# Loading the expert weights with each partition's rows 128 apart instead of adjacent, and transposing contiguous columns instead of strided ones

## The chip, the core and the metric

One Trainium2 chip, one core. The metric is the device time in microseconds of one execution of the whole program, median of the runs given.

## The reference, cut to what matters

The program computes two transformer-like blocks on 256 tokens of width 1024, all in float32. Only the last part of the second block is touched: a mixture of experts with 32 experts, of which each token uses 4.

```
def moe(h, router_w, router_b, w_up, b_up, w_down, b_down):
    logits = (xt @ router_w + router_b)
    top_vals, top_idx = lax.top_k(logits, TOP_K)          # 4 of 32
    gates = jax.nn.softmax(top_vals, axis=-1)
    ...
    def expert_block(args):                               # for each expert e and its tokens
        hcat = xblk @ w_up[e] + b_up[e]                   # [1024] -> [2048]
        x_glu = jnp.minimum(hcat[:, 0::2], SWIGLU_LIMIT)
        x_lin = jnp.clip(hcat[:, 1::2], -SWIGLU_LIMIT, SWIGLU_LIMIT)
        act = x_glu * jax.nn.sigmoid(SWIGLU_ALPHA * x_glu) * (x_lin + 1.0)
        return act @ w_down[e] + b_down[e]                # [1024] -> [1024]
```

Each expert has 8 MB of w_up and 4 MB of w_down, 402.7 MB over the 32 experts (192 panels of 2,097,152 bytes), and each byte is read once.

## The kernel before

Engines run side by side and meet at semaphores. All large weights pass through one ring in SBUF of six slots, each a "panel" of 2 MB (128 partitions of 16 KB). In the first 61 panels (the dense layers, four slots of the ring) a weight matrix is read as 512 columns, so that a partition's 16 KB come in eight pieces of 2 KB, or as 512 rows, in four pieces of 4 KB; both use the pattern `(k p) n -> p k n`, where the rows that one partition holds are 128 apart.

The expert stage (`moe_pe`, `moe_act`, `moe_dve`, `moe_sp`) is a hardware loop over e = 0 to 31 on each engine. An expert has six panels, j = 0 to 3 for w_up (256 rows of 2048 each) and j = 4, 5 for w_down (512 rows of 1024 each). SyncE issues them in that order at line 1923; before each it waits (line 1921) until TensorE has counted up `consumed` for the panel that held the slot. Here the rearrangement is `(p k) n`: partition p holds rows that are adjacent in the matrix, two of 8 KB or four of 4 KB, so 16 KB in one piece.

TensorE does for expert e, in this order (`dense`): the bias of the up product; the four up panels, 64 slots of tokens at a time, the two halves of the output on two halves of the array side by side (`halves`, lines 1535 and 1536); the gather of expert e+1's token rows; the first half of the scatter of expert e-1's result; four transposes of the activation `glu` (line 1522), whose first one also frees a slot; four transposes of the gathered rows of expert e+1 (line 1516); the first down panel; the second half of the scatter; the second down panel; two transposes of the weighted one-hot matrix (line 1529). ScalarE copies the transposed activation out of PSUM (line 1737) before the down product may start, and the transposed rows (line 1740) before the next expert's up product. A weight matrix laid out as `(p k)` needs inputs in the same order. So the transposes take every fourth column of `glu` and every second column of the rows: the columns that belong to panel row r. In a transpose the data is the weight load (PEld in the profile) and the identity matrix is the moving operand.

An expert that more than 64 tokens chose gets an extra pass over its panels (`one_pass`), during which no slot is freed until the pass is through with it. With these inputs that happens once, for expert 21.

The views and rows of the ring are made by these lines:

```
self.order = [4, 5] + [(PANELS + r) % RING for r in range(RING)]
self.panel = [k.ring[:, slot, :].rearrange("p (k n) -> p k n", k=2 if j < 4 else 4)
              for j, slot in enumerate(self.order)]
```

Of the kernel before, what the change touches and what calls it, by code (L numbers as in the profile page):

```python
# [21 lines left out]
P = 128  # L22
# [1479 lines left out]
def moe_pe(k, m):  # L1502
    nc, M, s = k.nc, k.nc.tensor, k.s

    def gather():

        for tt in range(TT):
            last = halves(m.XR, m.one_hot[:, tt, :], [k.x[:, tt, c:c + 512] for c in (0, 512)],
                          start=(tt == 0), stop=(tt == TT - 1))
        return last  # L1510

    def transpose_rows():

        for n in range(4):
            at = 256 * (n // 2) + n % 2
            last = M.transpose(m.XT[:, n * P:(n + 1) * P], m.xrows[:, at:at + 255:2], k.ident[:])
        return last

    def transpose_activated(frees):

        for n in range(4):
            last = M.transpose(m.AT[:, n * P:(n + 1) * P], m.glu[:, n::4], k.ident[:])  # L1522
            if n == 0 and frees:
                last.then_inc(s.consumed, 1)
        return last

    def transpose_weighted(frees):
        for tt in range(TT):
            last = M.transpose(m.AT[:, tt * P:(tt + 1) * P], m.weighted[:, tt, :], k.ident[:])
            if tt == 0 and frees:  # L1530
                last.then_inc(s.consumed, 1)
        return last
# [5 lines left out]
    def up_bias():  # L1538
        for q in range(2):
            halves(m.U[:, q, :], m.brow_of[:], [m.brow[:, c:c + 512] for c in (512 * q, D + 512 * q)],  # L1540
                   start=True, stop=False)

    def up_panel(inp, j):
        for r in range(2):
            for q in range(2):
                last = halves(m.U[:, q, :], inp[:, (2 * j + r) % 4, (2 * j + r) // 4, :],
                              [m.panel[j][:, r, c:c + 512] for c in (512 * q, D + 512 * q)],
                              start=False, stop=(j == 3 and r == 1))
        return last

    def down_panel(j):
        for r in range(4):
            c = 4 * j + r
            last = halves(m.DN, m.actT[:, r, j * SLOTS:(j + 1) * SLOTS],
                          [m.panel[4 + j][:, r, c0:c0 + 512] for c0 in (0, 512)], start=(c == 0), stop=(c == KD - 1))
        return last

    def scatter_tile(tt, matrix, rows):
        for half in range(2):
            r = slice(half * SLOTS, (half + 1) * SLOTS)  # L1560
            last = M.matmul(m.S[:, half, :], matrix[r, tt * P:(tt + 1) * P], rows[r, :], start=True, stop=True)  # L1561
        return last
# [8 lines left out]
    for tt in range(TT):  # L1571
        for c in range(KD):
            last = M.matmul(W[:, tt, 0:NE], k.hT[:, c, tt * P:(tt + 1) * P], m.rw[:, c, :], start=(c == 0), stop=(c == KD - 1))
# [10 lines left out]
    M.wait_ge(s.built, 2)  # L1584
    gather().then_inc(s.gathered, 1)
    M.wait_ge(s.rows_copied, 1)
    transpose_rows().then_inc(s.rows_T, 1)

    M.wait_ge(s.gate_ready, 1)
    for tt in range(TT):  # L1590
        last = M.transpose(m.S[0:NE, 0, tt * P:(tt + 1) * P], m.gate[:, tt, 0:NE], k.ident[:])
# [3 lines left out]
    for tt, ps in enumerate((m.S, k.psA[:, 2:4, :])):  # L1595
        for half in range(2):
            last = M.matmul(ps[:, half, :], m.gT[:, tt * P:(tt + 1) * P], m.bdown[:, half * 512:(half + 1) * 512],
                            start=True, stop=True)
# [5 lines left out]
    with M.Fori(0, NE) as e:  # L1604

        def panel_in(j):
            slot = m.order[j]
            before = 0 if slot >= RING else (PANELS - 1 - slot) // RING + 1
            M.wait_ge(s.panel_in[slot], 16 * (before + 1) + e * 16)

        def dense(free):
            M.wait_ge(s.gather_copied, 1 + e)
            M.wait_ge(s.u_taken, 1 + e)
            M.wait_ge(s.selected, 1 + e)
            up_bias()
            for j in range(3):
                panel_in(j)
                last = up_panel(m.xg, j)
                if free:
                    last.then_inc(s.consumed, 1)  # L1620
            panel_in(3)
            up_panel(m.xg, 3).then_inc(s.up_done, 1)
            M.wait_ge(s.built, 4 + e * 2)
            M.wait_ge(s.rows_copied, 1 + e)
            gather().then_inc(s.gathered, 1)
            M.wait_ge(s.y_copied, 1 + e)
            M.wait_ge(s.scatter_copied, 1 + e)
            M.wait_ge(s.summed, 1 + e * 2)
            scatter_tile(0, m.scatter, m.y).then_inc(s.scattered, 1)
            M.wait_ge(s.activated, 2 + e)  # L1630
            transpose_activated(free).then_inc(s.act_T, 1)
            M.wait_ge(s.rows_copied, 2 + e)
            transpose_rows().then_inc(s.rows_T, 1)
            M.wait_ge(s.act_copied, 2 + e)
            panel_in(4)
            last = down_panel(0)
            if free:
                last.then_inc(s.consumed, 1)
            M.wait_ge(s.summed, 2 + e * 2)
            scatter_tile(1, m.scatter, m.y).then_inc(s.scattered, 1)  # L1640
            panel_in(5)
            down_panel(1).then_inc(s.down_done, 1)
            M.wait_ge(s.gated, 3 + e * 2)
            transpose_weighted(free).then_inc(s.gated_T, 1)

        tokens = nc.values_load(m.cnt[0:1, bass.ds(e, 1)], min_val=0, max_val=T, engines=[M.engine])
        with M.If(tokens < SLOTS + 1):
            dense(True)
        with M.Else():
            dense(False)  # L1650

        def one_pass(i):
            dve_step = lambda n: extra_step(s, "dve", e, i, n)
            act_step = lambda n: extra_step(s, "act", e, i, n)

            def free_two(step):

                M.wait_ge(*extra_step(s, "pe", e, i, step))
                M.sem_inc(s.settled, 1)
                with M.If(tokens < 2 * SLOTS + 1):  # L1660
                    M.sem_inc(s.consumed, 2)

            M.wait_ge(*dve_step(2))
            gather().then_inc(s.extra_pe, 1)
            M.wait_ge(*act_step(1))
            transpose_rows().then_inc(s.extra_pe, 1)
            M.wait_ge(*dve_step(3))
            M.wait_ge(*act_step(2))
            up_bias()
            up_panel(m.xg_x, 0)  # L1670
            up_panel(m.xg_x, 1).then_inc(s.extra_pe, 1)
            free_two(3)
            up_panel(m.xg_x, 2)
            up_panel(m.xg_x, 3).then_inc(s.extra_pe, 1)
            free_two(4)
            M.wait_ge(*dve_step(7))
            transpose_activated(False).then_inc(s.extra_pe, 1)
            M.wait_ge(*act_step(4))
            down_panel(0)
            down_panel(1).then_inc(s.extra_pe, 1)  # L1680
            free_two(6)
            M.wait_ge(*dve_step(10))
            M.wait_ge(*act_step(5))
            transpose_weighted(False).then_inc(s.extra_pe, 1)
            M.wait_ge(*act_step(6))
            scatter_tile(0, m.scatter_x, m.y_x).then_inc(s.extra_pe, 1)
            M.wait_ge(*dve_step(11))
            scatter_tile(1, m.scatter_x, m.y_x).then_inc(s.extra_pe, 1)

        extra_passes(M, s, e, tokens, "pe", one_pass)  # L1690
        with M.If(tokens > 2 * SLOTS):
            M.sem_inc(s.consumed, 6)
# [218 lines left out]
def moe_sp(k, m):  # L1911
    S, s = k.nc.sync, k.s
    w_up, w_down = k.a["expert_w_up_2"][0], k.a["expert_w_down_2"][0]
    S.wait_ge(s.late, LATE_MOE)
    with S.Fori(0, NE) as e:
        for j, slot in enumerate(m.order):
            if j < 4:
                source = w_up[bass.ds(e, 1), j * 256:(j + 1) * 256, :]
            else:
                source = w_down[bass.ds(e, 1), (j - 4) * 512:(j - 3) * 512, :]  # L1920
            S.wait_ge(s.consumed, PANELS - 5 + j + e * 6)
            S.sem_inc(s.settled, 1)
            S.dma_start(m.panel[j], source.rearrange("o (p k) n -> p (o k) n", p=P)).then_inc(s.panel_in[slot], 16)
    for tt in range(TT):
        S.wait_ge(s.ln_done, 2 + tt + 1)
        S.dma_start(k.out[0, tt * P:(tt + 1) * P, :], m.acc[:, tt, :]).then_inc(s.stored, 16)
    S.wait_ge(s.stored, 16 * TT)


def build(nc, ctx, arrays, out):  # L1930
# [49 lines left out]
    moe_pool(k, m)  # L1980
    moe_act(k, m)
    moe_pe(k, m)
    moe_dve(k, m)
    moe_sp(k, m)


# [26 lines left out]
```

## Time and profile before

| what | value |
|---|---|
| median of 3 runs | 1999.52 us (1998.67 to 2000.78) |
| the profiled execution | 1998.67 us, of which 1997.4 us from the first to the last instruction (the span) |
| TensorE busy | 1861.5 us, 93% of the span |
| VectorE, ScalarE busy | 615.5 us, 463.9 us |
| mean granted TensorE clock | 0.967 of full speed |
| moved by DMA | 536.95 MB, mean 269 GB/s over the span |
| expert stage | from about 966 us to the end |

The busy time of an engine is an average over stages with different limits. A timeline gives for each merged row its start, its length, engine, line, operation, operands and count, and in brackets the idle time before it with what ended it. A window gives the busy time of each engine in a stretch with the count of its instructions, then the granted clock (1.00 is full speed), the mean busy share of the 16 DMA engines (it can read a little over 1) and the rate.

### The profile page before, as it was taken

What the parts mean: (1) busy time and instruction counts of PE and PEld (TensorE: products, weight loads), DVE (VectorE), ACT (ScalarE), POOL (GpSimd) and SP (SyncE); (2) the same over time, 40 slices, a digit from 0 to 9 for tenths busy, and PEclk for the clock granted to TensorE, in tenths of its full rate; (3) what the DMA queues carried; (4) which work ended last, traced back from release to release, by engine and by line L of the source; (5) the groups of instructions that cost most, each with busy time, mean ns of one, the idle gap of its engine ahead of it and who ended that gap; (6) DMA issues with size and microseconds to landing.
All of it is one profiled execution on the core that took longest, in us unless ns stands there. A gap on an engine that the chain in (4) does not pass through costs nothing.

```text
span 1997.4 us, 22265 instructions
## 1 busy us (share of the span) xinstructions
PE 1861.5 (93%) x8651; PEld 1002.2 (50%) x8652; DVE 615.5 (31%) x790; ACT 463.9 (23%) x556; POOL 53.8 (3%) x63
## 2 busy tenths in 40 slices
PE   7989998987999999998579999999999997999996
PEld 6769994474799877554323333333333332333332
DVE  4444442242544403551312212221222121222223
ACT  1435440131444313230101111111111110111111
POOL 0000001000000110220000000000000000000000
PEclk9989998999999999998689999999999998999998
DMA  7334543412354533230769999999999976999994
GB/s 259 142 138 170 207 171 99 155 43 81 130 197 183 174 126 119 92 127 0 305 270 429 429 428 429 428 429 429 428 429 429 428 311 252 395 429 429 428 429 180
DMA packets 84809, 536.95 MB, mean 269 GB/s; under 512 B 8688, under 2 KB 8792, under 8 KB 60152
## 3 DMA queue, kind: packets, MB, share of 16 engines
q1 hardware_dynamic: 79088, 531.64, 65.7%
q10 hardware_dynamic: 5672, 4.59, 0.9%
q8 instruction: 38, 0.62, 0.1%
q14 instruction: 11, 0.09, 0.0%
HBM read 535.17 MB, written 1.05 MB: 268 GB/s over the span
## 4 chain that ended last, share of the span: by engine, by line
PE 82%; DVE 8%; DMA 5%; ACT 2%; issue 2%; ACTq 0%; POOL 0%; PEldq 0%; DVEq 0%; SPq 0%; POOLq 0%
PE psA L1535 34%; PE psB L669 9%; PE psA L680 9%; PE psB L340 6%; PE psA L353 6%; PE psB L331 6%; DMA panel_ring<-in_expert_w_up 4%; PE psA L1065 2%; PE psB L1561 2%; PE psA L1522 1%; DVE linear L1866 1%; DVE glu L1869 1%; DVE glu L1863 1%; DVE linear L1864 1%; ACT activated_T L1737 1%
## 5 line engine op out<-in xcount | busy, mean ns | idle before, releaser
L1535 PE MATMUL psA<-panel_ring,gathered_T 128*64 128x512 f32 x1024 | 446.1, 593 | 2.4 <-DMA panel_ring<-in_expert_w_up 2.4
L1536 PE MATMUL psA<-panel_ring,gathered_T 128*64 128x512 f32 x1024 | 446.1, 593 | 0.0
L1535 PEld LDWEIGHTS psA<-panel_ring,gathered_T 128*64 128x64 f32 x1024 | 140.2, 137 | 296.8 <-issue 288.9
L1535 PE MATMUL psA<-panel_ring,activated_T 128*64 128x512 f32 x528 | 242.8, 603 | 7.3 <-ACT activated_T L1737 6.6
L1536 PE MATMUL psA<-panel_ring,activated_T 128*64 128x512 f32 x528 | 242.8, 603 | 0.0
L566 DVE TENSOR_TENSOR w_low<-panel_ring,w_high 128x2048 fp32r<-128x2048 f32 x64 | 146.5, 2292 | 171.8 <-ACT w_high L612 171.8
L1863 DVE TENSOR_SCALAR glu<-psA 128x512 f32<-128x512 f32 x32 | 22.1, 692 | 492.5 <-PE psA L1536 492.5
L612 ACT ACTIVATE w_high<-panel_ring 128x2048 fp32r<-128x2048 f32 x64 | 122.5, 1917 | 178.9 <-PE psB L669 104.9
L669 PE MATMUL psB<-hT_high,w_high 128*128 128x256 f32 x512 | 145.0, 283 | 2.0 <-DVE w_low L566 2.0
L669 PE MATMUL psB<-hT_low,w_high 128*128 128x256 f32 x512 | 144.9, 283 | 0.0
L669 PE MATMUL psB<-hT_high,w_low 128*128 128x256 f32 x512 | 144.9, 283 | 0.0
L1535 PEld LDWEIGHTS psA<-panel_ring,activated_T 128*64 128x64 f32 x528 | 67.5, 138 | 153.5 <-issue 139.7
L1536 PEld LDWEIGHTS psA<-panel_ring,gathered_T 128*64 128x64 f32 x1024 | 140.2, 137 | 0.0
L1819 DVE TENSOR_TENSOR moe_sum<-moe_sum,psB 128x1024 f32<-128x1024 f32 x68 | 82.8, 1218 | 168.7 <-PE psB L1561 168.7
L1732 ACT ACTIVATE swish_gate<-glu 128x512 f32<-128x512 f32 x32 | 20.1, 629 | 470.0 <-DVE glu L1863 470.0
L340 PE MATMUL psB<-panel_ring,hT 128*128 128x512 f32 x288 | 126.8, 601 | 1.3 <-DVE hT L304 1.3
L331 PE MATMUL psB<-hT,panel_ring 128*128 128x256 f32 x512 | 111.7, 379 | 2.7 <-DVE hT L1224 1.4
L331 PEld LDWEIGHTS psB<-hT,panel_ring 128*128 128x128 f32 x512 | 97.0, 190 | 16.5 <-DVE hT L1224 1.8
L669 PEld LDWEIGHTS psB<-hT_high,w_high 128*128 128x128 f32 x512 | 98.3, 192 | 3.8 <-issue 3.6
L680 PE MATMUL psA<-w_high,aT_high 128*128 128x512 f32 x256 | 99.7, 389 | 0.0
L680 PE MATMUL psA<-w_low,aT_high 128*128 128x512 f32 x256 | 99.7, 389 | 0.0
L680 PE MATMUL psA<-w_high,aT_low 128*128 128x512 f32 x256 | 99.6, 389 | 0.0
(392 smaller groups left out, 2375.9 us busy)
## 6 DMA issues: line engine op xcount, KB each, us to landing
panel_ring<-in_expert_w_up SPq DMA_DIRECT2D x128, 2048.0 KB, 14.8
panel_ring<-in_expert_w_down SPq DMA_DIRECT2D x64, 2048.0 KB, 15.0
panel_ring<-in_mlp_w SPq DMA_DIRECT2D x32, 2048.0 KB, 8.1
panel_ring<-in_w_in SPq DMA_DIRECT2D x11, 2048.0 KB, 7.9
panel_ring<-in_fox_w_in SPq DMA_DIRECT2D x6, 2048.0 KB, 7.8
panel_ring<-in_lru_w_in SPq DMA_DIRECT2D x4, 2048.0 KB, 16.8
panel_ring<-in_lru_w_out SPq DMA_DIRECT2D x2, 2048.0 KB, 7.8
panel_ring<-in_fox_w_out SPq DMA_DIRECT2D x2, 2048.0 KB, 8.6
```

What stands on the lines that cost most here:

```text
L331: last = M.matmul(out[:, m, :], w[:, c, m * P:(m + 1) * P], k.hT[:, c, :], start=(c == 0), stop=(c == KD - 1))
L340: last = M.matmul(ps[:, tt, :], k.hT[:, c, tt * P:(tt + 1) * P], w[:, c, :], start=(c == 0), stop=(c == KD - 1))
L353: mm = M.matmul(k.psA[:, 2 * tt + half, :], aT[:, c, tt * P:(tt + 1) * P], w[:, c, half * 512:(half + 1) * 512], start=first and c == 0, s ...
L566: rest = V.tensor_tensor(to(t.w[i % 2][1][:]), view, to(t.w[i % 2][0][:]).bitcast(F32), ALU.subtract)
L612: A.activation(to, view, ACT.Copy).then_inc(s.w_high, 1)
L669: last = M.matmul(out[:, 2 * (i % 2) + m, :], w[p][:, c, m * P:(m + 1) * P], h[q][:, c, :], start=(c == 0 and p == q), stop=(c == KD - 1 a ...
L680: last = M.matmul(k.psA[:, 2 * tt + half, :], at[p][:, 2 * (i % 2) + c, tt * P:(tt + 1) * P], w[q][:, c, half * 512:(half + 1) * 512], sta ...
L1065: last = M.matmul(ps[:, tt, :], k.hT[:, c, tt * P:(tt + 1) * P], wj[:, c, :], start=(c == 0), stop=(c == KD - 1))
L1535: M.matmul(ps[0:SLOTS], lhsT, rhs[0], **flags)
L1536: return M.matmul(ps[SLOTS:P], lhsT, rhs[1], **flags)
L1819: return V.tensor_tensor(m.acc[:, tt, :], m.acc[:, tt, :], flat(m.S[:]), ALU.add)
L1863: V.tensor_scalar(m.glu[:], even, SWIGLU_LIMIT, None, ALU.min).then_inc(s.glu_made, 1)
```

## The change

The expert panels are read with `(k p) n` instead of `(p k) n`: partition p now holds rows p and p+128 of the 256 rows of a w_up panel, and rows p, p+128, p+256, p+384 of the 512 rows of a w_down panel. The slot, the panel's size, the number of loads and their order stay as they were. The inputs of the products are put in the matching order by transposing contiguous blocks of 128 columns of the rows and of `glu`. The numbers of transposes, weight loads and matmuls, their shapes, and all waits stay as they were; two helper functions become one.

```
-    def transpose_rows():
-        for n in range(4):
-            at = 256 * (n // 2) + n % 2
-            last = M.transpose(m.XT[:, n * P:(n + 1) * P], m.xrows[:, at:at + 255:2], k.ident[:])
-        return last
-
-    def transpose_activated(frees):
-        for n in range(4):
-            last = M.transpose(m.AT[:, n * P:(n + 1) * P], m.glu[:, n::4], k.ident[:])
-            if n == 0 and frees:
-                last.then_inc(s.consumed, 1)
-        return last
+    def transposed(ps, src):
+        for n in range(4):
+            last = M.transpose(ps[:, n * P:(n + 1) * P], src[:, n * P:(n + 1) * P], k.ident[:])
+        return last
...
-            transpose_activated(free).then_inc(s.act_T, 1)
+            for n in range(4):
+                last = M.transpose(m.AT[:, n * P:(n + 1) * P], m.glu[:, n * P:(n + 1) * P], k.ident[:])
+                if free and n == 0:
+                    last.then_inc(s.consumed, 1)
+            last.then_inc(s.act_T, 1)
             M.wait_ge(s.rows_copied, 2 + e)
-            transpose_rows().then_inc(s.rows_T, 1)
+            transposed(m.XT, m.xrows).then_inc(s.rows_T, 1)
...
-            S.dma_start(m.panel[j], source.rearrange("o (p k) n -> p (o k) n", p=P)).then_inc(s.panel_in[slot], 16)
+            S.dma_start(m.panel[j], source.rearrange("o (k p) n -> p (o k) n", p=P)).then_inc(s.panel_in[slot], 16)
```

The calls ahead of the loop and in the extra pass are changed in the same way.

## Rows read from the trace of the kernel before

**Rows 1.** Page: PE busy time, and GB/s moved in 40 slices.
```profile
PE 1861.5 (93%) x8651; PEld 1002.2 (50%) x8652; DVE 615.5 (31%) x790; ACT 463.9 (23%) x556; POOL 53.8 (3%) x63
...
GB/s 259 142 138 170 207 171 99 155 43 81 130 197 183 174 126 119 92 127 0 305 270 429 429 428 429 428 429 429 428 429 429 428 311 252 395 429 429 428 429 180
```

**Rows 2.** Windows, one expert each: busy by engine, clock, DMA share, GB/s.
```profile
1301.90:1330.40 28.50, 28.22 (x132) 9.61 (x130) 6.21 (x11) 4.46 (x7) 0.00 (x0) 1.00 1.01 429
1559.80:1589.10 29.30, 28.43 (x132) 9.49 (x130) 6.20 (x11) 4.46 (x7) 0.00 (x0) 1.00 1.01 428
```

**Rows 3.** Timeline of the SyncE queue: start us, length, loads issued (merged).
```profile
1044.96 13.85 SPq L1923 DMA_DIRECT2D panel_ring<-in_expert_w_up  x4
...
1073.51 13.85 SPq L1923 DMA_DIRECT2D panel_ring<-in_expert_w_up  x4
...
1501.71 13.99 SPq L1923 DMA_DIRECT2D panel_ring<-in_expert_w_up  x4
...
1559.75 14.67 SPq L1923 DMA_DIRECT2D panel_ring<-in_expert_w_up  x4
...
1589.12 14.67 SPq L1923 DMA_DIRECT2D panel_ring<-in_expert_w_up  x4
...
1699.54 13.85 SPq L1923 DMA_DIRECT2D panel_ring<-in_expert_w_up  x4
```

**Rows 4.** Ring tile, the one issue at 1044.96: us from issue to landing.
```profile
DMA to landing us min/median/max: 7.5/7.5/7.5
```

**Rows 5.** Ring tile, the one issue near 1603.8: us from issue to landing.
```profile
DMA to landing us min/median/max: 22.2/22.2/22.2
```

**Rows 6.** Timeline of TensorE: the last matmul that a load released.
```profile
1625.70 0.64 PE L1535 MATMUL psA<-panel_ring,gathered_T 128*64 128x512 f32 x1 [0.60 <-DMA panel_ring<-in_expert_w_up]
```

**Rows 7.** Page: DMA packets by size.
```profile
DMA packets 84809, 536.95 MB, mean 269 GB/s; under 512 B 8688, under 2 KB 8792, under 8 KB 60152
```

**Rows 8.** Windows amid loading: four with 4 KB packets, two 2 KB, one 16 KB.
```profile
833.60:837.20 3.60, 3.60 (x10) 1.69 (x9) 3.40 (x2) 0.16 (x1) 3.36 (x1) 1.00 1.02 419
850.90:854.40 3.50, 3.50 (x10) 1.59 (x9) 3.30 (x2) 0.17 (x1) 3.25 (x1) 1.00 1.02 421
868.30:871.80 3.50, 3.50 (x10) 1.59 (x9) 3.39 (x2) 0.08 (x1) 3.35 (x1) 1.00 1.01 413
481.80:485.80 4.00, 4.00 (x11) 1.74 (x10) 0.00 (x0) 0.00 (x0) 0.00 (x0) 1.00 1.01 403
714.50:718.80 4.30, 4.30 (x22) 3.78 (x21) 0.00 (x0) 0.00 (x0) 0.00 (x0) 1.00 1.01 388
268.00:272.20 4.20, 4.20 (x38) 4.20 (x37) 2.29 (x1) 0.36 (x2) 0.00 (x0) 1.00 0.97 371
966.90:996.40 29.50, 18.96 (x75) 14.50 (x76) 11.78 (x34) 2.71 (x7) 0.00 (x0) 0.56 1.01 428
```

**Rows 9.** Groups of weight loads of transposes, expert stage: mean ns last before the bar.
```profile
L1516 PEld LDWEIGHTS psB<-ident,gathered_rows 128*128 128x128 f32 x132 | 18.8, 209 | 2.4 <-ACT gathered_rows L1750 2.4
L1522 PEld LDWEIGHTS psA<-ident,glu 128*128 128x128 f32 x132 | 18.6, 210 | 32.5 <-DVE glu L1869 28.6 <-DVE glu L1890 3.9
...
L1529 PEld LDWEIGHTS psA<-ident,gated_one_hot 128*128 128x128 f32 x66 | 6.6, 141 | 28.0 <-issue 26.0 <-ACT extra_out L1758 2.0
```

**Rows 10.** Timeline of one expert: transposes, copy, first down matmul.
```profile
1314.77 0.56 PEld L1522 LDWEIGHTS psA<-ident,glu 128*128 128x128 f32 x4 [0.90 <-DVE glu L1869]
...
1315.36 0.64 PE L1516 MATMUL psB<-ident,gathered_rows 128*128 128x128 f32 x4
...
1315.56 0.60 ACT L1737 ACTIVATE activated_T<-psA 128x512 f32<-128x512 f32 x1 [1.27 <-PE psA L1522]
...
1316.21 0.64 PE L1535 MATMUL psA<-panel_ring,activated_T 128*64 128x512 f32 x1 [0.21 <-ACT activated_T L1737]
```

**Rows 11.** Matmuls of two lines, 1300 to 1500: duration ns min/median/max.
```profile
L1522 PE MATMUL psA<-ident,glu x28: 283/285/386, 1314.8 to 1486.5; 128*128 128x128 f32 x28
...
L1529 PE MATMUL psA<-ident,gated_one_hot x14: 272/300/329, 1324.4 to 1495.9; 128*128 128x128 f32 x14
```

More of the change, by code:

```diff
@@ L1630, in dense @@
             M.wait_ge(s.activated, 2 + e)
-            transpose_activated(free).then_inc(s.act_T, 1)
+            for n in range(4):
[3 more added lines that the diff above has]
+            last.then_inc(s.act_T, 1)
             M.wait_ge(s.rows_copied, 2 + e)
-            transpose_rows().then_inc(s.rows_T, 1)
+            transposed(m.XT, m.xrows).then_inc(s.rows_T, 1)
             M.wait_ge(s.act_copied, 2 + e)
@@ L1665, in one_pass @@
             M.wait_ge(*act_step(1))
-            transpose_rows().then_inc(s.extra_pe, 1)
+            transposed(m.XT, m.xrows).then_inc(s.extra_pe, 1)
             M.wait_ge(*dve_step(3))
@@ L1676, in one_pass @@
             M.wait_ge(*dve_step(7))
-            transpose_activated(False).then_inc(s.extra_pe, 1)
+            transposed(m.AT, m.glu).then_inc(s.extra_pe, 1)
             M.wait_ge(*act_step(4))
```

## The prediction

> **What bounds the kernel now.** I read the page first. TensorE is busy 93% of the span, and over the expert stage the DMA rate stands flat at 428 to 429 GB/s [rows 1]. Two engines near their limit at once, so the busy shares cannot say which one sets the time. The windows of single experts can: an early one takes 28.50 us with TensorE busy for 28.22, a late one 29.30 us with TensorE busy for 28.43, and the DMA share is 1.01 in both [rows 2].
>
> The queue's timeline gives the exact periods. From the issue for expert 2 (1044.96) to that for expert 18 (1501.71) 16 periods pass, 28.547 us each. From 1559.75 to 1589.12 it is 29.37 us [rows 3]. A load of six panels is 12.583 MB; at 428.6 GB/s that is 29.36 us, 4.893 us a panel. So the DMA engines need 0.81 us more per expert than TensorE does, and the ring hides it at first. The landing times show how: with an idle queue a panel lands after 7.5 us [rows 4], late in the stage only after 22.2 us [rows 5]. Each expert adds 0.81 us of backlog until the six slots can hide no more. That cover is 16 x 0.81 plus about 0.7 in the 17th period: 13.7 us. From about expert 19 on TensorE waits for w_up panels; the last such wait ends at 1625.70 [rows 6].
>
> A check of this reading: the panel waited for there is up panel 3 of expert 21, the 118th from 1044.96 (19 experts of six and four more). 7.5 less one panel's 4.9 leaves 2.6 us of start; 1044.96 + 2.6 + 118 x 4.893 = 1624.9, and 1625.7 was seen. So up to there (segment A) the time is set by DMA alone, however fast TensorE is. Then expert 21's extra pass stops the loads, the queue runs empty, and expert 23's start at 1699.54 [rows 3] with full cover again. In segment B, the last 8.7 experts of loads, the backlog grows to 8.7 x 0.81 = 7.1 us, under 13.7. There TensorE sets the time.
>
> **Part 1, the loads: pieces of 8 and 4 KB in place of 16 KB.** The page counts 84809 packets, 60152 of them under 8 KB [rows 7]. The other 24657 are, within 81, the 192 x 128 = 24576 partitions of expert panels: one packet each. Afterwards a w_up panel has 256 packets and a w_down panel 512, that is 8 and 24 more for each of the 16 DMA engines. The order in HBM changes too, but the 4 KB panels of the dense layers have exactly the new w_down pattern, with pieces 512 KB apart.
>
> What a piece costs must come from those layers. In windows inside their loads, DMA share at or above 1.01, the four 4 KB panels moved 419, 421, 413 and 403 GB/s, on average 414; expert 0's 16 KB panels moved 428 [rows 8]. At 414 a panel takes 5.066 us, 0.173 more than 4.893, or 7.2 ns for each of 24 extra pieces. For 8 KB there is no row. Taking the same price per piece gives 8 x 7.2 ns = 0.058 us a panel, between nothing (as 16 KB) and what 2 KB pieces suggest: at 371 GB/s [rows 8] 0.76 us for 56 extra pieces, 13.6 ns each, so 0.109. I take 0.058, since 8 KB lies between sizes that both have rows and 4 KB is the nearer priced one. Per expert: 4 x 0.058 + 2 x 0.173 = 0.58 us, DMA period 29.94.
>
> Where it lands: in segment A in full, 19 x 0.58 + 4 x 0.058 = 11.2 us. The cover is used up sooner (growth 1.39 us plus part 2's gain, so after about nine experts, near 1310), but the last landing moves by just this sum. In B the growth is 8.7 x 1.39 = 12.1 us, still under 13.7: nothing. It would begin to cost there at 0.77 us more per expert. Before 1044.96 loads are ahead of TensorE, and in the dense layers nothing is changed.
>
> The Trainium skill (DMA: Bandwidth & Descriptors, "Why small descriptors are slow (HBM only)") also speaks against small pieces, but more mildly: about three cycles for each packet beside one cycle for each 32 bytes. By that, an estimate, 4 KB pieces cost 524/515 and 8 KB pieces 518/515 of 16 KB ones, 0.285 us per expert, and the whole would come to +4 us in place of +10.
>
> **Part 2, the transposes: contiguous weight loads.** The 128x128 loads with stride take 209 ns (every second column) and 210 ns (every fourth); those of the weighted one-hot, contiguous and of the same shape, 141 ns [rows 9]. Eight per expert are changed. The four of the gathered rows lie in cover: they end at 1316.00, while the copy of the transposed activation that the down product waits for runs to 1316.16, and the product starts at 1316.21 [rows 10]. The copy of the rows behind it is wanted only an expert later. The four of `glu` are on TensorE's path, since the copy starts when they end. Their loads pipeline: four take 0.56 us, not 0.84 [rows 10], so mostly the first counts, 0.07 us; the longest matmul of the burst, 386 ns, would fall towards the contiguous 329 [rows 11], about the same 0.06, and a little of the cadence goes too. I take 0.09 us per expert, between nothing (all hidden) and 4 x 0.07 = 0.28.
>
> It counts only where TensorE sets the time: experts 22 to 31, the first two, the extra pass and expert 21's end, 14 bursts: 14 x 0.09 = 1.3 us. In A it only lets TensorE wait sooner. The slot freed by the first transpose comes a few hundredths earlier; it shortens no load.
>
> The Trainium skill (SBUF — State Buffer, "Door 1: The DMA port swizzle", its note on cachelines) says that float32 reads may stride up to four elements for free; by that this part is worth nothing and the sum is +11.2. The rows disagree, 209 and 210 against 141 ns.
>
> **The sum.** +11.2 - 1.3 = +9.9 us. The profiled execution took 1998.67 us (span 1997.4, 1.3 us around it), so it would take 2008.6; it is 0.85 below the median, which goes to 1999.52 + 9.9 = 2009.4 us.
>
> **Rivals.** (1) Pieces are cheap: the best 4 KB row, 421 GB/s [rows 8], prices them at 0.088 us a panel and 0.029 for 8 KB, 0.29 per expert: 5.7 - 1.3, so 2003.9 us. If 8 KB costs nothing beside it, 0.176 per expert and 2001.5; if nothing costs anything, 1998.2. The flat 388 and 371 GB/s of 2 KB pieces speak against a price of nothing. That packets do not get smaller at all belongs here: the dense layers' counts speak against it.
> (2) w_up streams much worse, for instance as slowly as w_in's 2 KB panels, 388 GB/s [rows 8], because its partitions now jump 1 MB between pieces. Then it costs 4 x 0.51 + 2 x 0.173 = 2.4 us per expert: A 19 x 2.4 + 2 = 47.6, B 8.7 x 3.2 - 13.7 = 14.1, in all about +60, 2060 us. Against it: the dense panels jump too and reach 421.
> (3) Faster: smaller pieces stream better amid the busy ring than 16 KB ones. TensorE would then set the time throughout: it gets back the 2.3 us that it waits for DMA in A (19.7 x 0.81 - 13.7) and 33 x 0.09 = 3.0, so 1994.2 us. It decides where a panel's time falls by (2.3 + 1.8)/118 = 0.035 us, from 432 GB/s on. No window with small packets shows over 421.
>
> **Chances.** A measurement of this kernel can tell about 0.2%, 4 us, from no change. My forecast, an added DMA time of 0.3 to 1.1 us per expert: 0.62, all slower. Rival 1: 0.22, of which 0.05 slower and 0.17 within 0.2%. Rival 2: 0.10. Rival 3: 0.06. So slower 0.77, same 0.17, faster 0.06. The forecast's own high end takes 4 KB at 403 GB/s (0.31 us a panel) and 8 KB at 0.109: 1.06 per expert, A 20.6, B 8.7 x 1.87 - 13.7 = 2.6, less 1.3: 2021.4; its low end is 2004. The range has to reach into rival 1: 2000 to 2023, which leaves out rivals 2 and 3 and a part of 1.
>
> **What would show it.** Packets: 40960 more, about 125,800, 92,900 of them under 8 KB. The expert stage's rate near 420 GB/s in its full slices. Issue periods about 28.45 us up to expert 11, then 29.9 until expert 21; in segment B 28.45 throughout and landing times that reach about 20 us. Loads of the eight transposes near 141 ns. The wait that ended at 1625.70 ends 11 us later. Wrong would be: periods that stay at 29.4 late in A (pieces free), a rate below 410 (rival 2), waits for DMA in segment B, or weight loads still at 209 ns.

## The result and the profile after

The changed kernel takes 2013.76 us (median of 4 runs, 2011.98 to 2017.22) where the kernel before takes 1999.11 us (4 runs): a ratio of 1.0074, 95% interval 1.0056 to 1.0092. It is slower by 14.7 us. The prediction was 2009.4 us, between 2000 and 2023, slower with a chance of 0.77. The profiled execution took 2012.58 us, its span 2011.3 against 1997.4.

The page of the changed kernel, to set beside [rows 1] and [rows 7]: busy time of TensorE, the DMA rate in 40 slices, packets by size.

```profile
PE 1859.9 (92%) x8651; PEld 995.5 (49%) x8652; DVE 615.2 (31%) x790; ACT 463.9 (23%) x556; POOL 53.8 (3%) x63
...
GB/s 263 141 131 174 203 176 111 133 42 84 143 193 186 155 125 126 125 85 0 307 333 417 418 418 417 419 417 417 419 418 417 419 325 250 378 417 417 419 417 225
DMA packets 125769, 536.95 MB, mean 267 GB/s; under 512 B 8688, under 2 KB 8792, under 8 KB 92920
```

The packets are as forecast: 40960 more in all, 32768 more under 8 KB (the w_down panels; the 8 KB packets of w_up are not "under 8 KB"). The bytes are the same. TensorE's busy time is 1.6 us shorter, and the rate in the expert stage is 417 to 419 GB/s, where it was 428 to 429.

The SyncE queue's timeline of the changed kernel, for [rows 3]; the difference of two neighbouring starts is one expert's period.

```profile
1044.04 13.84 SPq L1917 DMA_DIRECT2D panel_ring<-in_expert_w_up  x4
...
1271.66 13.84 SPq L1917 DMA_DIRECT2D panel_ring<-in_expert_w_up  x4
...
1300.12 14.94 SPq L1917 DMA_DIRECT2D panel_ring<-in_expert_w_up  x4
...
1540.54 15.51 SPq L1917 DMA_DIRECT2D panel_ring<-in_expert_w_up  x4
...
1570.66 15.49 SPq L1917 DMA_DIRECT2D panel_ring<-in_expert_w_up  x4
...
1712.67 13.84 SPq L1917 DMA_DIRECT2D panel_ring<-in_expert_w_up  x4
...
1741.13 13.84 SPq L1917 DMA_DIRECT2D panel_ring<-in_expert_w_up  x4
```

The period is 28.45 us at first (the nine from 1044.04 to 1300.12 average 28.453), one of 29.55 follows, and then 30.12 us. The kernel before held 28.55 until expert 18, took 28.68 once and then 29.36. In the changed kernel the period is 28.45 again after the extra pass, from 1712.67 on. (Segment A is the stretch up to expert 21's last wait for a load, segment B the one from expert 23's issue to the end.) Two windows, one expert each, as in [rows 2]:

```profile
1540.54:1570.66 30.12, 28.48 (x132) 9.27 (x130) 6.20 (x11) 4.47 (x7) 0.00 (x0) 1.00 1.02 418
1741.13:1769.58 28.45, 28.13 (x132) 9.47 (x130) 6.21 (x11) 4.47 (x7) 0.00 (x0) 1.00 1.02 418
```

Both keep the DMA engines wholly busy (share 1.02) at 418 GB/s. In the first, TensorE is busy for 28.48 of 30.12 us and idles for the rest; in the second it is busy for 28.13 of 28.45 us, because the ring still has cover.

The landing time of the panel that TensorE waits for at the end of segment A, as in [rows 5]:

```profile
DMA to landing us min/median/max: 23.0/23.0/23.0
```

TensorE's timeline has this panel's first matmul, for [rows 6]:

```profile
1638.96 0.64 PE L1525 MATMUL psA<-panel_ring,gathered_T 128*64 128x512 f32 x1 [1.33 <-DMA panel_ring<-in_expert_w_up]
```

And near the end it has a wait that the kernel before does not have:

```profile
1976.68 0.64 PE L1525 MATMUL psA<-panel_ring,gathered_T 128*64 128x512 f32 x1 [1.31 <-DMA panel_ring<-in_expert_w_up]
```

The weight loads of the transposes, for [rows 9]: both strided groups have come down from 209 and 210 to 142 and 140 ns.

```profile
L1514 PEld LDWEIGHTS psB<-ident,gathered_rows 128*128 128x128 f32 x132 | 15.4, 142 | 2.4 <-ACT gathered_rows L1744 2.4
L1622 PEld LDWEIGHTS psA<-ident,glu 128*128 128x128 f32 x128 | 13.4, 140 | 28.6 <-DVE glu L1863 28.6
L1519 PEld LDWEIGHTS psA<-ident,gated_one_hot 128*128 128x128 f32 x66 | 6.7, 140 | 28.0 <-issue 26.0 <-ACT extra_out L1752 2.0
```

And one expert's timeline, for [rows 10]: from the first load to the start of ScalarE's copy it is 0.70 us (1314.11 to 1314.81), where it was 0.79 (1314.77 to 1315.56); the four loads take 0.42 us in place of 0.56. The product starts 0.04 us after the copy's end, where it was 0.05.

```profile
1314.11 0.42 PEld L1622 LDWEIGHTS psA<-ident,glu 128*128 128x128 f32 x4 [0.89 <-DVE glu L1863]
...
1314.61 0.60 PE L1514 MATMUL psB<-ident,gathered_rows 128*128 128x128 f32 x4
...
1314.81 0.60 ACT L1731 ACTIVATE activated_T<-psA 128x512 f32<-128x512 f32 x1 [1.17 <-PE psA L1622]
...
1315.45 0.64 PE L1525 MATMUL psA<-panel_ring,activated_T 128*64 128x512 f32 x1 [0.25 <-ACT activated_T L1731]
```

### The profile page after: what moved, and what is told of

Read it like the earlier page. It is cut to its first block, busy times and chain, and to the rows that moved or that the text cites. A ratio compares the mean times of both kernels' runs of the same rounds, so it can differ in the third digit from the quotient of the medians.

```text
span 2011.3 us, 22265 instructions
## 1 busy us (share of the span) xinstructions
PE 1859.9 (92%) x8651; PEld 995.5 (49%) x8652; DVE 615.2 (31%) x790; ACT 463.9 (23%) x556; POOL 53.8 (3%) x63
## 4 chain that ended last, share of the span: by engine, by line
PE 72%; DMA 15%; DVE 8%; ACT 2%; issue 2%; ACTq 0%; POOL 0%; PEldq 0%; SPq 0%; DVEq 0%; POOLq 0%
PE psA L1525 25%; DMA panel_ring<-in_expert_w_up 15%; PE psB L669 9%; PE psA L680 9%; PE psB L340 6%; PE psA L353 6%; PE psB L331 6%; PE psA L1065 2%; PE psB L1551 1%; DVE glu L1863 1%; DVE linear L1860 1%; DVE glu L1857 1%; DVE linear L1858 1%; PE psA L1622 1%; PE psB L732 1%
```

## Experiments

Whole times of this kernel scatter by several us from run to run (the kernel before: 1995.34 to 2002.70 in 25 runs beside the first four experiments). So each verdict rests on the periods in the queue's timeline of one trace per version. Where periods are even, they stay within 0.02 us of their mean in a trace, and the kernels that load alike agree across traces (late in segment A, where the loads set the time, 29.35 to 29.38 us with 16 KB pieces and 30.10 to 30.14 with the changed loads).

The traces also show one place where whole times differ by more than the changes account for: the stretch from expert 21's last wait to expert 23's issue, in which the extra pass runs and TensorE has gaps. It took 73.8 us at a mean granted clock of 0.88 before, 72.6 us at 0.91 with w_up alone and with w_down alone, 76.8 us at 0.82 with the transposes alone, and 74.7 us at 0.86 in the last version below, which has the same loads and the same periods as that.

### Loads alone, transposes alone

The first has only the new order of the loads:

```
-            S.dma_start(m.panel[j], source.rearrange("o (p k) n -> p (o k) n", p=P)).then_inc(s.panel_in[slot], 16)
+            S.dma_start(m.panel[j], source.rearrange("o (k p) n -> p (o k) n", p=P)).then_inc(s.panel_in[slot], 16)
```

> Only the loads are changed (rows 128 apart); the transposes keep their strided columns, so the products get their inputs in the old order and the values are not the reference's. Theory (the cost is in the loads alone): expert periods late in segment A as in the changed kernel, 30.12 us, and in segment B as before, 28.55 us; in all +14.7 us against the kernel before. Rival (strided weight loads and small pieces disturb each other, or part of the loss came with the transposes): a period other than 30.1 in A, or other than 28.55 in B.

Measured: 2015.03 us (4 runs) against 1998.56, ratio 1.0082 (1.0057 to 1.0106), +16.5 us. Its queue, late in A and then in B:

```profile
1540.50 15.46 SPq L1923 DMA_DIRECT2D panel_ring<-in_expert_w_up  x4
...
1570.62 15.47 SPq L1923 DMA_DIRECT2D panel_ring<-in_expert_w_up  x4
...
1741.90 13.89 SPq L1923 DMA_DIRECT2D panel_ring<-in_expert_w_up  x4
...
1770.45 13.89 SPq L1923 DMA_DIRECT2D panel_ring<-in_expert_w_up  x4
```

30.12 and 28.55 us, as the theory had it. Up to expert 21's last wait, counted from expert 2's issue, the loads alone cost 14.0 us (594.78 against 580.74) and the whole change 14.2: the loads hold the whole loss.

The second is the changed kernel with the old order of the loads (the line above the other way round).

> Only the transposes are changed to contiguous columns; the loads keep 16 KB pieces, so the values are not the reference's. Theory: weight loads of the eight transposes at 141 ns, periods of 28.455 us while TensorE sets the time, 29.36 us once the cover is used up in A, and -1.3 us in all (14 bursts of 0.09 us); where DMA sets the time the gain is lost. Rival (TensorE's gain counts everywhere): 32 x 0.09 = -2.9 us. Rival (stride is free for the path): 28.55 us and no change.

Measured: 1997.48 us (10 runs) against 1998.56, ratio 0.9987 (0.9975 to 1.0000). Its queue:

```profile
1531.32 14.71 SPq L1917 DMA_DIRECT2D panel_ring<-in_expert_w_up  x4
...
1560.70 14.70 SPq L1917 DMA_DIRECT2D panel_ring<-in_expert_w_up  x4
...
1732.02 13.79 SPq L1917 DMA_DIRECT2D panel_ring<-in_expert_w_up  x4
...
1760.47 13.80 SPq L1917 DMA_DIRECT2D panel_ring<-in_expert_w_up  x4
```

And the first matmul of the panel that ends segment A, on TensorE's timeline:

```profile
1626.74 0.64 PE L1525 MATMUL psA<-panel_ring,gathered_T 128*64 128x512 f32 x1 [0.70 <-DMA panel_ring<-in_expert_w_up]
```

The period is 28.45 us in B and 29.38 late in A (29.35 to 29.38 over three periods). The gain of 0.09 us per expert is real, and where DMA sets the time it is lost: expert 21's last wait ends 580.5 us after expert 2's issue (1626.74 - 1046.21), where the kernel before has 580.7. The whole time of -1.1 us fits -1.3, but its interval fits -2.9 too; the periods decide against "it counts everywhere".

### w_up alone, w_down alone

In both, each product's inputs are in the order of its weights. The first has the new order in w_up and contiguous transposes of the rows, the second the new order in w_down and contiguous transposes of `glu`:

```
+            order = "o (k p) n -> p (o k) n" if j < 4 else "o (p k) n -> p (o k) n"    # w_up alone
+            order = "o (p k) n -> p (o k) n" if j < 4 else "o (k p) n -> p (o k) n"    # w_down alone
+            S.dma_start(m.panel[j], source.rearrange(order, p=P)).then_inc(s.panel_in[slot], 16)
```

> w_up in 8 KB pieces and the transposes of the rows contiguous; w_down and the transposes of the activation as before. Theory (a fixed price per piece; the changed kernel's 0.76 us per expert over 80 extra pieces for each DMA engine is 9.5 ns): 0.076 us a panel, late period in A 29.66 us, B 28.55 us because the rows' transposes lie in cover, total +6.1 us. Rival (8 KB pieces stream like 16 KB, all of the loss is in the 4 KB panels): 29.36 us and no change.

Measured: 2002.34 us (10 runs), +3.8; ratio 1.0011 (1.0000 to 1.0023).

```profile
1535.67 15.02 SPq L1923 DMA_DIRECT2D panel_ring<-in_expert_w_up  x4
...
1565.35 15.01 SPq L1923 DMA_DIRECT2D panel_ring<-in_expert_w_up  x4
...
1733.35 13.89 SPq L1923 DMA_DIRECT2D panel_ring<-in_expert_w_up  x4
...
1761.89 13.89 SPq L1923 DMA_DIRECT2D panel_ring<-in_expert_w_up  x4
```

The period late in A is 29.68 us (29.65 to 29.69 over six periods, mean 29.67), so 0.31 above 29.36 and 0.078 a panel. In B it is 28.54: the rows' transposes, now contiguous, bring nothing, since they lie in cover.

> w_down in 4 KB pieces and the transposes of the activation contiguous; w_up and the rows' transposes as before. Theory (9.5 ns per piece): 0.228 us a panel, late period in A 29.82 us, B 28.455 us, total 8.7 - 1.3 = +7.4 us. Rival (all of the loss is in the 4 KB panels): 30.12 us and +13.1 us. With the window price of the prediction, 7.2 ns per piece, 29.71 us and +5.3 us.

Measured: 2004.98 us (10 runs), +6.4; ratio 1.0026 (1.0015 to 1.0037).

```profile
1537.90 15.16 SPq L1924 DMA_DIRECT2D panel_ring<-in_expert_w_up  x4
...
1567.72 15.17 SPq L1924 DMA_DIRECT2D panel_ring<-in_expert_w_up  x4
...
1736.17 13.79 SPq L1924 DMA_DIRECT2D panel_ring<-in_expert_w_up  x4
...
1764.62 13.80 SPq L1924 DMA_DIRECT2D panel_ring<-in_expert_w_up  x4
```

The period late in A is 29.82 us (mean 29.83): 0.47 above 29.36, 0.235 a panel. In B it is 28.45: the gain of 0.09 us belongs to the `glu` transposes alone. The two prices add up: 0.31 + 0.47 = 0.78, against the changed kernel's 0.76. Per extra piece they are 0.078/8 = 9.7 ns and 0.235/24 = 9.8 ns. The whole times lie 2.3 and 1.0 us under the expectations, and the interval of w_up alone (0 to +4.6 us) leaves its +6.1 out. The traces show no such shortfall where the loads set the time: from expert 2's issue to expert 21's last wait the two take 5.95 and 8.50 us more than the 580.74 of the kernel before, together 14.45, against 14.2 for the whole change. Each then gets 1.3 us back in the stretch of the extra pass, at the higher granted clock told above. Whole times do not carry a verdict on 2 us here.

### Smaller pieces everywhere

The changed kernel with every expert panel in pieces of `PANEL // 4` floats (4 KB), and in a second run `PANEL // 8` (2 KB):

```
+            width = PANEL // 4
+            flat_rows = source.rearrange("o r (h n) -> o (r h) n", n=width) if source.shape[2] > width else source
+            S.dma_start(m.panel[j].rearrange("p k n -> p (k n)").rearrange("p (k n) -> p k n", n=width),
+                        flat_rows.rearrange("o (k p) n -> p (o k) n", p=P)).then_inc(s.panel_in[slot], 16)
```

> The changed kernel with all six panels of an expert read in 4 KB pieces, (k p) order with k = 4; the w_up values land in other places than the products want, so the output is not the reference's; bytes, waits and products are the same. Theory (9.7 ns per piece for each DMA engine, from 0.078 us a w_up panel and 0.235 us a w_down panel): 6 x 0.235 = 1.41 us, late periods of 30.77 us in segment A; in B growth of 8.7 x 2.3 = 20 us against 13.7 of cover, so waits there too; about +33 us in all. Rival (what costs is the jump of 1 MB or 512 KB, not the number of pieces: three jumps for one in w_up): the same sign, which the run with adjacent pieces tells apart.

Measured: 2027.35 us in one run beside 1999.32, +28 for an expected +33. The trace has +26.4 us in segment A and +4.8 in B, where TensorE waits for w_up panels as expected; it also has 1.1 us less ahead of expert 2 and 1.3 less in the stretch of the extra pass. The periods late in A are uneven, 31.06, 31.04, 31.03 and 29.75 us, and repeat every four experts. So the two rows below are four experts apart:

```profile
1396.48 20.46 SPq L1919 DMA_DIRECT2D panel_ring<-in_expert_w_up  x4
...
1519.36 20.46 SPq L1919 DMA_DIRECT2D panel_ring<-in_expert_w_up  x4
```

122.88/4 = 30.72 us, 1.36 above 29.36: 0.227 a panel, 9.4 ns per piece.

> As the run with 4 KB pieces, but all panels in 2 KB pieces (k = 8); the values again land elsewhere and the output is not the reference's. Theory (the price is per piece, 9.7 ns): 56 x 9.7 = 0.54 us a panel, periods of 32.6 us, 386 GB/s, about +84 us. Rival (the price per piece grows as pieces shrink, as the 371 GB/s window of the 2 KB dense panels said, 13.6 ns): 33.9 us.

Measured: 2083.40 us in one run, +84 as expected. Again four experts apart:

```profile
1424.88 22.88 SPq L1919 DMA_DIRECT2D panel_ring<-in_expert_w_up  x4
...
1554.98 22.88 SPq L1919 DMA_DIRECT2D panel_ring<-in_expert_w_up  x4
```

130.10/4 = 32.53 us, 3.17 above 29.36, 0.528 a panel, 9.4 ns per piece. The price per piece is flat from 8 KB down to 2 KB; the rival, 33.9 us because the price grows as pieces shrink, is out.

### The same pieces, adjacent in HBM

The changed kernel, but a partition's pieces are neighbours in the matrix and are put into the slot in reverse, so that they cannot become one packet:

```
-            S.dma_start(m.panel[j], source.rearrange("o (k p) n -> p (o k) n", p=P)).then_inc(s.panel_in[slot], 16)
+            S.dma_start(m.panel[j][:, ::-1, :], source.rearrange("o (p k) n -> p (o k) n", p=P)).then_inc(s.panel_in[slot], 16)
```

> The changed kernel, but each partition again reads adjacent rows, and puts them into its slot in reverse order, so that the pieces stay 8 KB and 4 KB (as many packets as in the changed kernel) while a partition's 16 KB lie together in HBM. The rows reach the products in another order than their inputs have, so the output is not the reference's. Theory (the number of pieces costs): late periods 30.12 us and the changed kernel's time. Rival (the order in HBM costs, jumps of 1 MB and 512 KB): 29.36 us and the time of the kernel before, less 1.3 us.

Measured: 2011.15 us in one run, span 2009.9. Its packets on the page, and two issues late in A:

```profile
DMA packets 125769, 536.95 MB, mean 267 GB/s; under 512 B 8688, under 2 KB 8792, under 8 KB 92920
```

```profile
1540.32 15.66 SPq L1917 DMA_DIRECT2D panel_ring<-in_expert_w_up  x4
...
1570.43 15.68 SPq L1917 DMA_DIRECT2D panel_ring<-in_expert_w_up  x4
```

The same packets as in the changed kernel and 30.11 us (30.11 to 30.14). Without the jumps in HBM the cost is the same, so the number of pieces costs, and the order of rows does not.

### Contiguous transposes with 16 KB pieces

The experiments point to a version with the old loads of the panels and contiguous weight loads of `glu`. The order must then change somewhere on the way to `glu`. First at VectorE's write of the product:

```
-        V.tensor_tensor(m.glu[:], m.lin[:], m.sig[:], ALU.mult).then_inc(s.activated, 1)
+        V.tensor_tensor(by_row(m.glu), natural(m.lin), natural(m.sig), ALU.mult).then_inc(s.activated, 1)
...
+    by_row = lambda t: t[:].rearrange("p (n s) -> p s n", n=4)
+    natural = lambda t: t[:].rearrange("p (s n) -> p s n", n=4)
```

> The kernel before with 16 KB pieces, and the product that makes glu written by VectorE in the order that lets its transposes load contiguous columns; the rows' transposes keep their stride, since they lie in cover. Theory: loads of the glu transposes at 141 ns, periods of 28.455 us where TensorE sets the time, 29.36 us once the cover is used up, VectorE's product still about 0.69 us; -1.3 us in all, hardly to be told from no change in whole times, but plain in the periods. Rival (a write with a stride of 512 bytes slows VectorE's product, which is on the path): the period grows by what the product grows, above 28.55 us.

Measured: 2002.64 us (11 runs) against 1999.32, ratio 1.0015 (1.0004 to 1.0025). The rival held. VectorE's product in this run, then the same product in the kernel before:

```profile
L1871 DVE TENSOR_TENSOR glu<-linear,swish_gate 128x512 f32<-128x512 f32 x32 | 33.4, 1044 | 1.1
...
L1869 DVE TENSOR_TENSOR glu<-linear,swish_gate 128x512 f32<-128x512 f32 x32 | 22.1, 691 | 1.1
```

Two issues late in A:

```profile
1537.40 14.15 SPq L1925 DMA_DIRECT2D panel_ring<-in_expert_w_up  x4
...
1566.20 14.15 SPq L1925 DMA_DIRECT2D panel_ring<-in_expert_w_up  x4
```

The strided write takes 1044 ns, where the product took 691. It lies on TensorE's path: 28.545 + 0.353 - 0.09 = 28.81 us, the period seen from the start to the end. The loads never come to set the time in segment A: their backlog grows by 29.36 - 28.81 = 0.55 us per expert, so the cover of 13.7 us would last for 25 experts.

Then at the two clamps, which read PSUM with a stride in any case:

```
-    even, odd = (flat(m.U)[:, i::2] for i in range(2))
+    even, odd = (flat(m.U)[:, i::2].rearrange("p (s n) -> p n s", n=4) for i in range(2))
+    in_order = lambda t: t[:].rearrange("p (n s) -> p n s", n=4)
...
-        V.tensor_scalar(m.glu[:], even, SWIGLU_LIMIT, None, ALU.min).then_inc(s.glu_made, 1)
+        V.tensor_scalar(in_order(m.glu), even, SWIGLU_LIMIT, None, ALU.min).then_inc(s.glu_made, 1)
...
-            last = M.transpose(m.AT[:, n * P:(n + 1) * P], m.glu[:, n::4], k.ident[:])
+            last = M.transpose(m.AT[:, n * P:(n + 1) * P], m.glu[:, n * P:(n + 1) * P], k.ident[:])
```

> The kernel before with 16 KB pieces; VectorE's two clamps read the up product from PSUM in the order of the panel rows (a step of eight floats in place of two) and write glu and linear without a stride, so that everything after them, the glu transposes too, is contiguous. The result is the reference's. Theory (a strided read from PSUM costs VectorE no more at eight than at two, about 0.69 us each): periods of 28.455 us where TensorE sets the time, 29.36 us once the cover is used up in A, -1.3 us in all, plain in the periods and hardly in whole times. Rival (the wider step slows the clamps as the strided write slowed the product, 0.35 us each): periods of about 29.1 us and +10 us or more in all.

Measured: 1998.82 us (12 runs) against 2000.18, ratio 0.9996 (0.9983 to 1.0009). The two clamps in the groups of the expert stage:

```profile
L1864 DVE TENSOR_SCALAR glu<-psA 128x512 f32<-128x512 f32 x32 | 22.2, 692 | 493.8 <-PE psA L1536 493.8
...
L1865 DVE TENSOR_SCALAR linear<-psA 128x512 f32<-128x512 f32 x32 | 21.8, 681 | 0.0
```

The first clamp in the kernel before:

```profile
L1863 DVE TENSOR_SCALAR glu<-psA 128x512 f32<-128x512 f32 x32 | 22.1, 692 | 492.5 <-PE psA L1536 492.5
```

The queue:

```profile
1530.31 14.70 SPq L1924 DMA_DIRECT2D panel_ring<-in_expert_w_up  x4
...
1559.67 14.71 SPq L1924 DMA_DIRECT2D panel_ring<-in_expert_w_up  x4
...
1728.83 13.80 SPq L1924 DMA_DIRECT2D panel_ring<-in_expert_w_up  x4
...
1757.29 13.79 SPq L1924 DMA_DIRECT2D panel_ring<-in_expert_w_up  x4
```

The clamps take 692 and 681 ns, where they took 692 and 680 with a step of two. The periods are 29.36 us late in A and 28.46 in B; no other version has shorter ones. As a whole time its gain cannot be told from nothing.

## Why the prediction was right, point by point

**Which engine sets the time where.** Right, and it carried the rest. Segment A ends with a wait for expert 21's up panel 3 in both kernels. The two profiled executions, stretch by stretch in us, with what the prediction's sum has there:

| stretch | before | after | difference | forecast |
|---|---|---|---|---|
| up to expert 2's issue | 1044.96 | 1044.04 | -0.9 | -0.2 |
| from there to expert 21's last wait (A) | 580.74 | 594.92 | +14.2 | +11.2 |
| from there to expert 23's issue | 73.8 | 73.7 | -0.1 | -0.2 |
| from there to the end (B) | 297.9 | 298.6 | +0.8 | -0.9 |
| span | 1997.4 | 2011.3 | +13.9 | +9.9 |

The forecast's own mechanism thus missed by +3.0 in A and +1.7 in B. Of the -0.9 ahead of expert 2's issue, 0.56 us had come about before the first expert load (965.93 before, 965.37 after), where nothing was changed: that is scatter, and it happens to bring the sum nearer to the forecast.

**The price of a piece.** This term was mis-sized, and with it most of the difference between +9.9 and +14.7. The prediction took 7.2 ns, from windows of 3.5 to 4 us in the dense layers [rows 8]; the runs show 9.4 to 9.8 ns at 8, 4 and 2 KB. The four windows price a piece anywhere from 3.7 ns (421 GB/s) to 13 ns (403 GB/s), so that their mean came within a quarter of the truth is partly luck. The step from the 4 KB price to 8 KB ("the same price per piece") was right in kind: 0.078 us a panel for the 0.058 forecast, at the right ratio to 0.235, for which 0.173 stood. So 0.76 us per expert in place of 0.58. With the measured prices the prediction's own sum for A is 80 x 0.078 + 38 x 0.235 = 15.2 us; 14.2 came. The prediction's check put the wait of the kernel before 0.8 us too early (1624.9 for 1625.7), and with the measured prices the same check puts that of the changed kernel 0.2 us too late (1639.2 for 1638.96); the two make up the missing us, and why they differ stays open. The mean of the small windows was too high a rate and so too low a price: 414 GB/s, where the long row of 4 KB pieces (the run with 4 KB everywhere) gives 410. At 2 KB one of the two windows, 371 GB/s, was far too low, and the other, 388, close to the 387 of a long row. Whether short windows or the dense layers themselves make the difference was not tested.

**The page's price.** The rule of about three cycles for each packet (the Trainium skill, DMA: Bandwidth & Descriptors, "Why small descriptors are slow (HBM only)") made 0.285 us per expert of it. The measured 0.76 is 2.7 times that; that small pieces cost at all, and in proportion to their number, agrees with the runs.

**The transposes.** Right in kind and size: 28.45 us for 28.545, from the `glu` transposes alone. The hundredth is luck. The prediction named 0.07 us for the first load and 0.06 for the longest matmul, and chose 0.09 without working out how much of each counts. The whole -1.3 us could not be checked in whole times. The rule that a float32 read may stride up to four elements for free (the Trainium skill, SBUF — State Buffer, "Door 1: The DMA port swizzle", its note on cachelines) does not hold for these weight loads: 209 and 210 ns with stride, 140 to 142 without.

**Segment B.** Wrong: it was forecast as free of waits, and a wait for DMA there is one of the signs that the prediction lists as wrong. The limit, "0.77 us more per expert", was compared with the mis-sized 0.58, and it left out that TensorE's gain makes the backlog grow too: 8.7 x (0.81 + 0.76 + 0.09) = 14.4 us against 13.7 of cover. So TensorE waits once, at the last up panel, which lands 23.4 us after its issue where the prediction had about 20. The run with the loads alone bears this out: without the gain its backlog grows by 8.7 x 1.57 = 13.7 us, and its profile shows no matmul that waits for a load in segment B. The changed kernel's segment B is 2.5 us longer than the 296.1 of the transposes alone, which has the same gain and no wait. Of this, 0.95 us lies in the last four scatter matmuls, which took 2.08 us at a granted clock of 0.50 and 1.13 us at 1.00; the other 1.5 us is the wait, more than the 0.7 by which 14.4 exceeds 13.7. The kernel before took 1.90 us for these four matmuls, at 0.56. So the +0.8 adds up as -0.9 for ten bursts, +1.5 for the wait and +0.2 for the clock.

**The rivals.** Cheap pieces (+4 us) fell with the loads alone. That w_up streams much worse because its partitions jump 1 MB fell twice: its price per piece is that of w_down, and adjacent pieces cost the same. That smaller pieces stream faster fell with 418 GB/s where 16 KB pieces had 428.

**Open.** Why a piece costs 9.4 to 9.8 ns was not looked into; what the runs show is that neither its size from 2 to 8 KB nor its place in HBM matters. Whether it is the read from HBM or the write to the slot that costs was not told apart either: in every run both sides were cut into the same pieces.

## What to carry to other kernels

Look at what hides a cost, and for how long. Here a queue that needs 3% more time than the engine behind it is invisible for 17 experts and sets the time after them. So a change of 0.76 us per expert cost 14 us and not 24, and a faster TensorE gained nothing where the loads set the time. A faster engine also uses the cover up sooner, which is what brought the wait in segment B. A weight layout that gives each partition one long run is worth a stride elsewhere, but choose where: a stride in a PSUM read that was strided anyway cost nothing, the same order made by a strided write cost 0.35 us each time. Price a rate from a long stretch: the mean of four windows of four microseconds was off by 1%, which was a quarter of the price.

## What the hardware showed that was not expected

In these loads from HBM each further packet costs a DMA engine 9.4 to 9.8 ns beside its bytes, for 2, 4 and 8 KB pieces alike: 428, 410 and 387 GB/s at 16, 4 and 2 KB. VectorE's product of two 128x512 float32 tiles took 1044 ns with a write that steps by 512 bytes and 691 ns without, while its clamp reads PSUM at a step of eight floats in the same 692 ns as at two. And once a ring of six slots is short of loads, periods need not be even: with 4 KB pieces three of 31.0 us are followed by one of 29.75, with 2 KB pieces 34.23, 32.70, 32.69 and 30.49 us come in turn, and only their mean is the DMA engines' time. Two executions of one program part can differ by the clock alone: the same four scatter matmuls took 1.13 us at a granted clock of 1.00 and 2.08 us at 0.50.
